# The second segment's x, turned by the tensor engine or read already turned

## The reference, cut to what matters

```python
def rms_norm(x, w):
    xf = x.astype(jnp.float32)
    y = xf * lax.rsqrt(jnp.mean(xf * xf, axis=-1, keepdims=True) + EPS)
    return (y * w.astype(jnp.float32)).astype(x.dtype)
...
    h = rms_norm(x, norm_w) * (1.0 + scale[:, None]) + shift[:, None]
    proj = h @ w_in
...
    attn = sliding_window_attention(aq, ak, av, sinks) * jax.nn.silu(ag)
    rec = hgrn2_chunkwise(...)
    rec = rms_norm(rec, rec_norm_w).reshape(B, S, REC_WIDTH).astype(x.dtype)
    rec = rec * jax.nn.silu(rg)
    mixed = jnp.concatenate([attn, rec], axis=-1) @ w_out
    return x + gate[:, None] * mixed
```

## Time and profile before

| what | value |
|---|---|
| runs | 1829.62, 1830.82, 1832.54 us; median 1830.82 |
| span of the profiled execution | 1830.7 us |
| busy PE / DVE / ACT / POOL | 1796.6 / 1286.0 / 987.6 / 535.1 us |
| recurrence of segment 0 | from about 538 to 800 us of the span |

### The profile page before, as it was taken

The page is one execution under the profiler, slowest core; times in us unless marked ns, Lnnn a source line. Parts: engine busy times, 40 slices in busy tenths (PEclk is TensorE's granted clock), DMA queues, the critical chain, the costliest instruction groups (busy, mean ns, idle before and its releaser), DMA issues.

```text
span 1830.7 us, 29478 instructions
## 1 busy us (share of the span) xinstructions
PE 1796.6 (98%) x10368; PEld 1507.4 (82%) x10368; DVE 1286.0 (70%) x2628; ACT 987.6 (54%) x2127; POOL 535.1 (29%) x857
## 2 busy tenths in 40 slices
PE   6999999999999999999999999999999999999999
PEld 4788888888878888888888888887888888888887
DVE  7966467777766666697546677775775557987987
ACT  5622226877776565652222577777656555343341
POOL 1000026777723233210002567763333321000000
PEclk9999999999999999999999999999999999999999
DMA  9143232222222344344233222131432138278352
GB/s 356 69 162 114 93 121 87 74 74 58 63 96 85 118 137 120 113 167 161 81 121 106 100 74 75 39 87 33 175 99 78 62 131 304 106 251 286 112 178 92
DMA packets 158498, 222.37 MB, mean 121 GB/s; under 512 B 11792, under 2 KB 104336, under 8 KB 150672
## 3 DMA queue, kind: packets, MB, share of 16 engines
q1 hardware_dynamic: 158352, 220.49, 36.1%
HBM read 163.18 MB, written 57.28 MB: 120 GB/s over the span
## 4 chain that ended last, share of the span: by engine, by line
PE 89%; DVE 3%; DMA 3%; issue 2%; ACT 1%; POOL 1%; SPq 0%; DVEq 0%; POOLq 0%; ACTq 0%
PE bank L898 69%; PE bank L1055 3%; PE bank L1044 3%; PE bank L1076 3%; PE bank L1144 2%; PE bank L1128 2%; PE bank L1109 2%; PE bank L1102 1%; PE bank L1008 1%; DMA x_home<-in_x 1%; DMA raw<-in_w_in 1%; PE bank L1158 1%; PE bank L1133 1%; DMA h_f<-x_cols 1%; DVE g_lo L1802 0%
## 5 line engine op out<-in xcount | busy, mean ns | idle before, releaser
L898 PE MATMUL bank<-h_hi,w_hi 128*128 128x512 f32 x512 | 207.3, 405 | 0.2
L898 PE MATMUL bank<-h_lo,w_hi 128*128 128x512 f32 x512 | 200.4, 391 | 0.0
L898 PE MATMUL bank<-h_hi,w_lo 128*128 128x512 f32 x512 | 200.2, 391 | 0.0
L898 PE MATMUL bank<-wq_hi,h_hi 128*128 128x384 f32 x512 | 177.7, 347 | 0.5 <-issue 0.5
L898 PE MATMUL bank<-ob_hi,oa_hi 128*128 128x512 f32 x448 | 175.0, 391 | 0.0
L898 PE MATMUL bank<-ob_hi,oa_lo 128*128 128x512 f32 x448 | 174.4, 389 | 0.0
L898 PE MATMUL bank<-ob_lo,oa_hi 128*128 128x512 f32 x448 | 174.3, 389 | 0.0
L898 PE MATMUL bank<-wq_hi,h_lo 128*128 128x384 f32 x512 | 172.6, 337 | 0.0
L898 PE MATMUL bank<-wq_lo,h_hi 128*128 128x384 f32 x512 | 171.8, 336 | 0.0
L1326 ACT ACTIVATE g_hi<-g_raw 128x2048 fp32r<-128x2048 f32 x36 | 69.0, 1916 | 162.9 <-PE bank L898 155.8
L1485 ACT ACTIVATE sm<-sm,neg_m 128x257 f32<-128x257 f32 x256 | 127.4, 504 | 18.0 <-DVE neg_m L2051 17.9
(11 more groups left out here) (257 smaller groups left out, 4832.7 us busy)
## 6 DMA issues: line engine op xcount, KB each, us to landing
g_raw<-in_w_in SPq DMA_DIRECT2D x24, 1024.0 KB, 6.2
raw<-in_w_in SPq DMA_DIRECT2D x16, 1024.0 KB, 8.1
o_lower<-mixed_cols SPq DMA_DIRECT2D x32, 512.0 KB, 6.4
nat_rows<-u SPq DMA_DIRECT2D x48, 256.0 KB, 2.6
raw<-in_w_in SPq DMA_DIRECT2D x8, 1536.0 KB, 6.9
o_upper<-in_w_out SPq DMA_DIRECT2D x24, 512.0 KB, 8.7
wa<-in_w_ada SPq DMA_DIRECT2D x8, 1024.0 KB, 12.0
g_q<-gate_cols SPq DMA_DIRECT2D x64, 128.0 KB, 2.5
```

The lines of the kernel that those rows point to most:

```text
L898: mm = pe.matmul(dst, a, b, start=(first and m == 0), stop=(last and m == 2), **more)
```

## The change

The program gets x of segment 1 a second time, as an input `xT` that already has the features on the partitions. Its normalization needs the root of a token along the free axis now, the same row on all partitions. The sums of squares are still formed from `xb` in token rows. POOL's root of a block (128 values, one per partition) is written to a DRAM tensor `root_d` (in the profile `x_roots`), read back by a broadcasting DMA into `root_bc` (128 by 128), and POOL multiplies the turned block `xt` (128 by 1024) with it. The result goes to `x_T_d` as before, 512 KB in one DMA instead of 256 KB in two. The transposes on PE, the multiplication and the copies on DVE are gone. The three hand-written tables are gone too: block m is loaded in turn m-1, squared in turn m+1, its root is written in turn m+2, its turned form is loaded and multiplied in turn m+3 and written in turn m+4.

```diff
-        X_HALVES = [[], [], [0], [1], [2], [3, 4], [5], [6], [7, 8], [9], [10], [11, 12], [13], [14], [15]]
-        X_LOADS = {0: (0, 1), 4: (2,), 6: (3,), 7: (4,), 9: (5,), 10: (6,), 12: (7,)}
-        X_SQUARES = {1: 0, 3: 1, 4: 2, 6: 3, 7: 4, 9: 5, 10: 6, 12: 7}
+        X_BLOCKS = range(NBLK)
...
                 def load_x(m):
                     if m >= 2:
-                        sp.wait_ge(x_T, NBLK + 2 * (m - 1))
+                        sp.wait_ge(x_sqd, NBLK + 2 * (m - 1))
...
+                def spill_root(m):
+                    sp.wait_ge(x_rs, 2 * NBLK + 3 * (m + 1))
+                    sp.dma_start(root_d[m].unsqueeze(1), x_rinv[:, m:m + 1]).then_inc(root_out, 16)
+
+                def load_turned(m):
+                    sp.wait_ge(root_out, 16 * (m + 1))
+                    geq(sp, xt_out, 16 * m)
+                    sp.dma_start(root_bc[:], root_d[m].unsqueeze(0).to_broadcast([P, P])).then_inc(xt_in, 16)
+                    sp.dma_start(xt[:], xT[:, :, tokens(m)]).then_inc(xt_in, 16)
+
+                def spill_x(m):
+                    sp.wait_ge(x_nrm, NBLK + m + 1)
+                    sp.dma_start(x_T_d[:, :, tokens(m)], xt[:]).then_inc(xt_out, 16)
...
-                    if t >= 1:
-                        for half in x_halves(s, t - 1):
-                            spill_x(half)
                     if s + 1 < SEGS:
-                        for m in X_LOADS.get(t, ()):
-                            load_x(m)
+                        if t == 0:
+                            load_x(0)
+                        if x_block(s, t, 4) is not None:
+                            spill_x(t - 4)
+                        if x_block(s, t, 3) is not None:
+                            load_turned(t - 3)
+                        if x_block(s, t, 2) is not None:
+                            spill_root(t - 2)
+                        if t + 1 in X_BLOCKS:
+                            load_x(t + 1)
                         next_gemm(s, t)
...
-            def transpose_half(i):
-
-                m, half = i // 2, i % 2
-                pe.wait_ge(x_nrm, NBLK + m + 1)
-                pe.wait_ge(x_ev_v, X_DVE + i)
-                for k in range(KH):
-                    mm = pe.transpose(bank[6][:, k * P:(k + 1) * P], xb[m % 2][:, half * KH + k, :], ident[:])
-                mm.then_inc(x_T, 1)
...
-            def normalize_half(m):
-
-                dve.wait_ge(x_rs, 2 * NBLK + 3 * m + 3)
-                dve.tensor_scalar(xb[m % 2][:], xb[m % 2][:], x_rinv[:, 0:1], None, ALU.mult).then_inc(x_nrm, 1)
-
-            def copy_half(t):
-                dve.wait_ge(x_T, NBLK + t + 1)
-                geq(dve, xt_out[t % 2], 16 * (t // 2))
-                dve.tensor_copy(xt[t % 2][:].rearrange("p k t -> p (k t)"), bank[6][:, :]).then_inc(x_ev_v, 1)
...
+            def normalize_turned(m):
+
+                pool.wait_ge(xt_in, 32 * (m + 1))
+                pool.tensor_tensor(xt[:], xt[:], root_bc[:].unsqueeze(1).to_broadcast([P, KT, P]), ALU.mult
+                                   ).then_inc(x_nrm, 1)
```

More of the change, by code:

```diff
@@ L71, with hybrid_layer @@
 AT_RAW1 = AT_RAW + 3 * GQ * 4
-def hybrid_layer(nc, x, cT, pos, norm_w, w_ada, b_cols, b_gate, w_in, qk_w, sinks, rec_w, lbT, w_out,
-                 ident_d, masks_d, causal_d, freq_d, out, mixed_T, nat, gate_T, x_T_d, a21_d, carry_k, carry_v):
+def hybrid_layer(nc, x, xT, cT, pos, norm_w, w_ada, b_cols, b_gate, w_in, qk_w, sinks, rec_w, lbT, w_out,
+                 ident_d, masks_d, causal_d, freq_d, out, mixed_T, nat, gate_T, x_T_d, root_d, a21_d, carry_k, carry_v):
     with ExitStack() as ctx:
@@ L220, in hybrid_layer @@
         assert at <= AT_END - D * 4
-        (xt0, xt1), at = row(AT_XT, ("xt0", [P, KH, P], F32), ("xt1", [P, KH, P], F32))
+        (xt,), at = row(AT_XT, ("xt", [P, KT, P], F32))
         (x_half, g_ones, ga_sum), at = row(at, ("x_half", [P, 8], F32), ("g_ones", [P, P], F32),
@@ L224, in hybrid_layer @@
         assert at <= AT_S + 2 * 2 * GQ * 4
+        root_bc = place(at - HALF * 4, "root_bc", [P, P])
         s_in, e_b, q_dec, k_inv, k_out = [s_in0, s_in1], [e_b0, e_b1], [q_dec0, q_dec1], [k_inv0, k_inv1], [k_out0, k_out1]
-        r_v, rg_w, r_mix, xt = [r_v0, r_v1], [rg_w0, rg_w1], [r_mix0, r_mix1], [xt0, xt1]
+        r_v, rg_w, r_mix = [r_v0, r_v1], [rg_w0, rg_w1], [r_mix0, r_mix1]
         o_ss, o_var, o_rinv = o_ss[:], o_var[:], o_rinv[:]
@@ L312, in hybrid_layer @@
         stage_in = [sem(f"stage_in{i}") for i in range(2)]
-        xt_out = [sem(f"xt_out{i}") for i in range(2)]
+        root_out, xt_in, xt_out = sem("root_out"), sem("xt_in"), sem("xt_out")
         gate_in = sem("gate_in")
@@ L398, in comb, with x_block @@
             return 20 * n + kind[0] + kind[1] * c + 1
-        X_HALVES = [[], [], [0], [1], [2], [3, 4], [5], [6], [7, 8], [9], [10], [11, 12], [13], [14], [15]]
-        X_LOADS = {0: (0, 1), 4: (2,), 6: (3,), 7: (4,), 9: (5,), 10: (6,), 12: (7,)}
-        X_SQUARES = {1: 0, 3: 1, 4: 2, 6: 3, 7: 4, 9: 5, 10: 6, 12: 7}
-        def x_halves(s, t):
-            return X_HALVES[t] if s + 1 < SEGS and t < len(X_HALVES) else []
+        X_BLOCKS = range(NBLK)
+        def x_block(s, t, behind):
+            return t - behind if s + 1 < SEGS and t - behind in X_BLOCKS else None
         def w_use(s, r, index):
@@ L736, in next_gemm @@
                 if t == REC_T - 1:
-                    for half in range(2):
-                        sp.wait_ge(xt_out[half], 16 * NBLK)
+                    sp.wait_ge(xt_out, 16 * NBLK)
                     sp.wait_ge(rq_ok, base + REC_T - 1)
@@ L1231, in recurrence @@
                         chunk_products(s, T - 1, t - 1)
-                    for half in x_halves(s, t)[:1]:
-                        transpose_half(half)
                     if s + 1 == SEGS and t in (5, 7):
@@ L1527, in squares_done @@
             def squares_done(s, t):
-                return NBLK + 2 * sum(at < t for at in X_SQUARES) if s + 1 < SEGS else 0
+                return NBLK + 2 * min(max(t - 1, 0), NBLK) if s + 1 < SEGS else 0
             def mix_copy(s, t):
@@ L1634, in recurrence @@
                     if s + 1 < SEGS:
-                        if t in X_SQUARES:
+                        if x_block(s, t, 1) is not None:
                             geq(act, rgs_ok, T)
-                            square_half(X_SQUARES[t], QB * (T - 1))
+                            square_half(t - 1, QB * (T - 1))
                         if t == REC_T + 1:
@@ L2351, in recurrence @@
                         out_lo(0, 0, 2)
-                    for half in x_halves(s, t)[:1]:
-                        copy_half(half)
                     if s + 1 < SEGS and t == REC_T - 1:
@@ L2367, in recurrence @@
                         decay_q(s, t)
-                    for half in x_halves(s, t)[1:]:
-                        copy_half(half)
                     if s + 1 < SEGS and t == REC_T + 1:
@@ L2539, in recurrence @@
                         pool.tensor_tensor(k_out[b][:], k_f[:], k_out[b][:], ALU.mult).then_inc(kout_ok, 1)
-                    if s + 1 < SEGS and t in X_SQUARES:
-                        root_half(X_SQUARES[t])
+                    if x_block(s, t, 1) is not None:
+                        root_half(t - 1)
+                    if x_block(s, t, 3) is not None:
+                        normalize_turned(t - 3)
             for s in range(SEGS):
```

28 lines of the change are left out of this document (9 added, 19 removed).

## The result

The changed kernel takes 1839.09 us (median of four runs, 1836.28 to 1841.87) against 1830.77 us for the kernel before (a fourth run of it, 1830.72 us, stands beside the three above); the ratio is 1.0047, with a 95% interval of 1.0032 to 1.0061. It is 0.5% slower, where 1824.1 us was forecast. The profiled execution has a span of 1837.4 us, 6.7 us above the span of before. The run that it belongs to took 1839.23 us, 1.8 us more than its span, and every other run whose span is known lies 1.7 to 1.9 us above it too. So the trace of before, with 1830.7 us, most likely belongs to its slowest run, 1832.54 us, and not to one near the median.

A forecast was written before the change was run, and what follows sets the result against it. PE was taken to bound the kernel, busy 1796.6 of 1830.7 us (98%). Removed transposes give -6.7 us and the added POOL and SP work 0: 1830.8 - 6.7 + 0 = 1824.1 us, range 1822.4 to 1828.5.

The forecast's parts named there:

- the write of 128 roots of 4 bytes each: On SP's queue: root write and broadcast take between the fixed 2.0 us and 4.7 us, with a whole turn available.
- The sum for `rg_w`: SP's load behind xb and r_v: 593.9 + 2.0 + 4 x 0.87 = 599.4, 5.5 us after the first issue.
- a slack of 1.1: At chunk_products: o_T done at 601.66, wanted at 602.73, so rg_w may land about 1.1 us later before PE waits.
- 64 transposes are worth 6.7 us: On PE in segment 0: removing 16 groups of four transposes gives -6.7 us, bounds 5.8 to 6.9.
- POOL's multiplication, 2.1 to 2.6 us, four times hidden: One 128 by 1024 multiplication per block on POOL fits four times into its 10.40 us idle time before k_out.
- `rg_w` 5.5 us after the first issue, `k_f` just not late, PE without a wait: SP to ACT to PE: tanh ends at 600.0, k_f is released by PE at 600.06, adding 0 us.
- Rival (a), the gate rows come too late: rg_w lands late behind SP's loads, PE waits in five turns; 3.0 us lost, 1827.1 us; chance 0.11.
- Rival (b), the ring: SP and POOL's cycle of multiplication, write, wait, load makes xt late in turns 3 to 10; 1836 to 1840 us; chance 0.08.
- A wait of PE costs its length: On PE: rg_w landing x us late costs x - 1.1 in each of five turns, at most 0.6 x 5 = 3.0 us.

The follow-up runs named there:

- wide pieces: The changed kernel with its 4-byte root write replaced by equally many pieces of 512 bytes (a tile of ones), read back as root row; 1825.05 us, ratio 0.9976.
- the first experiment: The changed kernel with the 4-byte root write issued at the end of SP's turn, behind r_v, rg_w and the write of o_T; 1842.1 us, ratio 1.007.

## Why the prediction was wrong

The step that failed is the sentence on "the write of 128 roots of 4 bytes each": no row existed for it, and I bounded it by "nothing beyond the fixed 2.0 us" below and "the 4.7 us of the 512 KB load" above. It takes 9.6 us in the change and 8.9 us where it stands alone ahead of `rg_w`, outside both bounds, so the nearest row by kind of instruction was no bound. The bound would have held for a harmless write: with wide pieces, at the same place behind the load of `xt`, the median is 4.1 us. Worse, I looked only at who waits for it and not at what is queued behind it. The sum for `rg_w` counted four quarters of a megabyte and left out the half kilobyte ahead of them. With the measured landing it works out: the root write is issued at 591.2 and done 8.8 us later, at 600.0, most of the 1 MB is moved behind it, and the tanh starts at 604.65, where 5.5 us after the first issue (593.82) would have been 599.3. That is 5.3 us late, against a slack of 1.1 that turn 4, itself delayed, had already used up, and PE waits 5.36 us.

Point by point:

- *64 transposes are worth 6.7 us.* The turns confirm it: 16.12 to 16.14 us in all undisturbed turns, against 16.55 with one group. In runs the kernel with wide pieces gains 0.24%, 4.4 us, with an interval from 2.6 to 6.4, a little under the 6.7. Its span is 7.5 us shorter than the one of before, but that compares with a trace in which turn 2 took 17.70 us instead of the 16.1 of the same turn with 512-byte writes added: PE's clock was 0.50 from 544 to 547 us there. Where the last 2 us of the runs' median go I cannot show.
- *POOL's multiplication, 2.1 to 2.6 us, four times hidden.* It takes 2.39 us and was never ahead of a late `k_out`.
- *`rg_w` 5.5 us after the first issue, `k_f` just not late, PE without a wait.* Right to 0.1 us, once the root write is harmless. `k_f` then follows the tanh at once, and `o_T` is done at 599.33, 0.8 us before PE wants it at 600.12, where 1.1 was reckoned.
- *Rival (a), the gate rows come too late.* This is what happened, at the place and through the chain described, but with 10.8 us from the first issue to the tanh instead of the 7.2 that I gave as its longest. I gave it 0.11, and my longest case came out at 1827.1 us, still below the kernel before. Its reason, weights or `xt` still in flight, was not the one.
- *Rival (b), the ring.* Its time, 1836 to 1840, is the measured one, but not its mechanism: POOL waits 3.5 us for `xt` in all, and `b_cum` was never held. That the number fits is luck. POOL waited more, 6.8 us, in the first experiment, and not at all with wide pieces.
- *A wait of PE costs its length.* True for four of the five waits, up to the 3.0 us of turn 7. The wait of 5.36 us cost 8.16, because PE restarted at the lower clock.

## What to carry to other kernels

Count what a DMA does to the queue behind it, not only who waits for its landing, and take nothing for small because its bytes are few: a column of 4-byte values, one per partition, written packed to DRAM held the transfers of both queues for some 7 us (an estimate: its 9 us to landing less the fixed 2 of the prediction). Nor is a transfer safe by being issued ahead of it, if it is still in flight. To turn such a column into a row, let the pieces land in SBUF, or make the row on PE with a diagonal. And where a change needs one operation that the trace has no row for, measure that operation alone, added to the old kernel at the place where it would stand.

## What the runs showed of the hardware that I had not expected

128 pieces of 4 bytes, packed in DRAM, land after 8.4 to 9.7 us (medians of the five kernels that have them). The same pieces 512 bytes apart land after 1.4 us, packed pieces of 16 bytes after 1.4, and the 4-byte pieces packed in SBUF after 1.9. While the slow write is under way 33 to 46 GB/s are moved in the stretches shown, and a write issued by ACT holds the loads issued by SP as well.

The Trainium skill, DMA: Bandwidth & Descriptors, says in its specifications that pieces under 512 bytes are read, modified and written back. The runs agree that something sets small writes to DRAM apart, but not at that bound: 16 and 64 bytes packed cost no more than 512, and 4 bytes cost nothing when they do not stand side by side. Whether any of these writes reads and modifies first, no run here shows.

After a wait of 5.36 us PE's granted clock was 0.50, and eight small matmuls took 2.04 us instead of 1.16. The length of the wait alone does not tell it: after the 2.99 us of turn 7 the clock stayed at 1.00, while in the trace of before it was 0.50 from 544 to 547 us, shortly after a wait of 1.83 us that ended at 542.83, and that turn took 1.6 us longer. Eight waits with 26.6 us in all made the kernel before 41 us slower.
